# The order of TensorE's steps between two experts' gate and down products: token transposes ahead of and between the halves of down, scatter behind them

## The reference, cut to what matters

```python
def step(acc, xs):
    e, rt, rw = xs
    xb = xf[rt]
    hb = jax.nn.silu(xb @ w_gate[e]) * (xb @ w_up[e])
    yb = (hb @ w_down[e]).astype(F32) * rw[:, None]
    return acc.at[rt].add(yb), None
...
routed = routed_experts(xf, topi, topw, w_gate, w_up, w_down)
shared = (jax.nn.silu(xf @ sh_gate) * (xf @ sh_up)) @ sh_down
return (routed + shared).reshape(B, S, D)
```

## Time and profile before

| | us |
|---|---|
| median of 3 runs | 3258.38 (3256.17 to 3263.91) |
| profiled execution, device time | 3263.08 |
| its span, first to last instruction | 3261.8 |
| TensorE matmuls busy | 2954.0 (91%) |
| VectorE busy | 1182.2 (36%) |
| ScalarE busy | 478.6 (15%) |
| POOL busy | 102.7 (3%) |

### The profile page before, as it was taken

The page is one execution under the profiler, slowest core; times in us unless marked ns, Lnnn a source line. Parts: engine busy times, 40 slices in busy tenths (PEclk is TensorE's granted clock), DMA queues, the critical chain, the costliest instruction groups (busy, mean ns, idle before and its releaser), DMA issues.

```text
span 3261.8 us, 40722 instructions
## 1 busy us (share of the span) xinstructions
PE 2954.0 (91%) x15750; PEld 2104.0 (65%) x15750; DVE 1182.2 (36%) x2590; ACT 478.6 (15%) x1034; POOL 102.7 (3%) x98
## 2 busy tenths in 40 slices
PE   5998899999998899999689999998969689999998
PEld 4766677776666678878475555555858575555554
DVE  1435324433435324441335222224566235222223
ACT  1212210001212301000211111111220111111111
POOL 0000000000000000000001000000000001000000
PEclk9998899999998899999699999999979789999999
DMA  4222135562221146654219999995410119999995
GB/s 153 76 93 76 65 129 207 219 244 101 75 93 71 58 162 225 245 219 154 102 55 376 397 405 405 396 402 230 143 52 1 78 62 411 399 400 392 392 400 233
DMA packets 106612, 684.59 MB, mean 210 GB/s; under 512 B 19777, under 2 KB 21201, under 8 KB 25873
## 3 DMA queue, kind: packets, MB, share of 16 engines
q1 hardware_dynamic: 92384, 661.56, 52.1%
q0 software_dynamic: 11264, 16.54, 1.5%
q10 hardware_dynamic: 2864, 5.09, 0.4%
HBM read 703.57 MB, written 4.19 MB: 217 GB/s over the span
## 4 chain that ended last, share of the span: by engine, by line
PE 76%; DMA 11%; DVE 7%; ACT 3%; issue 1%; ACTq 1%; SPq 0%; DVEq 0%; POOLq 0%
PE PS L440 73%; DMA wmoe<-in_experts 11%; PE PS L445 3%; ACT AR L2013 2%; ACTq L2401 1%; SPq L2529 0%; DVE H L1182 0%; ACT AR L2063 0%; DVE wmoe L1716 0%; DVE H L1716 0%; ACT ST L2013 0%; DVE ST L1235 0%; DMA AR<-tokens,IX 0%; DVE wmoe L1255 0%; ACT wmoe L2013 0%
## 5 line engine op out<-in xcount | busy, mean ns | idle before, releaser
L440 PE MATMUL PS<-wmoe,AR 128*64 128x256 f32 (+1 forms) x5360 | 717.4, 424 | 36.7 <-DMA wmoe<-in_experts 22.6
L440 PE MATMUL PS<-H,wdense 128*128 128x256 f32 (+2 forms) x3056 | 720.5, 397 | 20.8 <-DVE H L1182 9.3
L440 PEld LDWEIGHTS PS<-H,wdense 128*128 128x128 f32 (+1 forms) x3056 | 595.2, 196 | 132.1 <-issue 17.4
L440 PEld LDWEIGHTS PS<-wmoe,AR 128*64 128x64 f32 x5360 | 385.2, 137 | 321.0 <-issue 145.9
L2013 ACT ACTIVATE AR<-PS 128x256 f32<-128x256 f32 (+4 forms) x512 | 231.7, 457 | 1768.4 <-PE PS L440 1159.1
L440 PE MATMUL PS<-AR,wdense 128*128 128x256 f32 (+1 forms) x1920 | 441.0, 391 | 35.7 <-DVE wmoe L1255 10.7
L440 PE MATMUL PS<-AR 128*128 128x512 f32 (+12 forms) x1492 | 413.6, 423 | 57.0 <-DVE AR L1242 13.9
L440 PEld LDWEIGHTS PS<-AR,wdense 128*128 128x128 f32 x1920 | 368.9, 193 | 105.0 <-issue 20.4
L440 PEld LDWEIGHTS PS<-AR 128*128 128x128 f32 (+6 forms) x1492 | 218.0, 200 | 159.5 <-issue 86.6
L445 PEld LDWEIGHTS PS<-CST,AR 128*128 128x128 f32 (+5 forms) x1158 | 132.7, 136 | 178.3 <-issue 137.8
L440 PE MATMUL PS<-wdense,H 128*128 128x256 f32 (+4 forms) x1024 | 219.8, 372 | 0.0
(11 more groups left out here) (286 smaller groups left out, 1580.8 us busy)
## 6 DMA issues: line engine op xcount, KB each, us to landing
wmoe<-in_experts SPq DMA_DIRECT2D x402, 1024.0 KB, 8.7
wdense<-in_dense SPq DMA_DIRECT2D x176, 1024.0 KB, 4.8
wmoe<-in_ada SPq DMA_DIRECT2D x48, 1024.0 KB, 7.0
tokens<-AR POOLq DMA_DIRECT2D x4, 512.0 KB, 3.8
wdense<-in_dense SPq DMA_DIRECT2D x2, 768.0 KB, 11.0
CST<-in_const ACTq DMA_DIRECT2D x1, 1389.0 KB, 20.7
wdense<-in_dense SPq DMA_DIRECT2D x2, 640.0 KB, 6.9
CST<-in_const ACTq DMA_DIRECT2D x1, 1136.0 KB, 15.1
```

Of the source, the lines that this page charges most:

```text
L440: return te.matmul(out, lhsT, rhs, start=start, stop=stop, skip_group_check=True)
```

## The change

The body of a pair is reordered on TensorE. `down` takes one half q at a time. x0 stands between gate_up and the first half of down, x1 between the halves, the first scatter behind the second half, the transposes of the hidden values behind it, then numbers and the second scatter. The event "added before", on which VectorE turns the weights of the last pair, is the second scatter, now the last event of a pair and no longer the one before the last. The other engines' programs are as they were; the counts on which they wait follow the new order.

```diff
-            def down(slots, what):
-                w = [slots(e, 2, D) for e in range(2)]
-                for q in range(2):
-                    for f in range(2):
-                        for e in range(2):
-                            m = mm(PS[e * CAP:(e + 1) * CAP, B_D[q], :], M_HB[:, f, e * CAP:(e + 1) * CAP],
-                                   w[e][:, f, 512 * q:512 * q + 512], start=f == 0, stop=f == 1)
-                    PE.up(m, *what, q)
+            def down(q, w, what):
+                for f in range(2):
+                    for e in range(2):
+                        m = mm(PS[e * CAP:(e + 1) * CAP, B_D[q], :], M_HB[:, f, e * CAP:(e + 1) * CAP],
+                               w[e][:, f, 512 * q:512 * q + 512], start=f == 0, stop=f == 1)
+                PE.up(m, *what, q)
...
-                PE.at[what + ("added before",)] = PE.n - 1
+                PE.at[what + ("added before",)] = PE.n
                 te.wait_ge(AC.sem, at(AC, what + ("x1 read before",)))
                 gate_up(lambda j, k, w: slots(j, k, w), what + ("gu",))
+                te.wait_ge(tokens_landed[L], landings)
+                gather(0, what + ("x0",))
+                w = [slots(4 + e, 2, D) for e in range(2)] if before else None
                 if before:
                     te.wait_ge(AC.sem, at(AC, what + ("turned before",)))
+                    down(0, w, what + ("d",))
+                te.wait_ge(AC.sem, at(AC, what + ("x0",)))
+                gather(1, what + ("x1",))
+                if before:
                     te.wait_ge(VE.sem, at(VE, what + ("numbers before",)))
-                    down(lambda j, k, w: slots(4 + j, k, w), what + ("d",))
-                te.wait_ge(tokens_landed[L], landings)
-                gather(0, what + ("x0",))
-                if before:
+                    down(1, w, what + ("d",))
                     te.wait_ge(VE.sem, at(VE, what + ("ye", 0)))
                     add_up(0, what + ("added",))
-                te.wait_ge(AC.sem, at(AC, what + ("x0",)))
-                gather(1, what + ("x1",))
+                te.wait_ge(VE.sem, at(VE, what + ("hidden",)))
+                turn_hidden(what + ("hb",))
                 te.wait_ge(VE.sem, at(VE, what + ("chosen",)))
                 if before:
                     te.wait_ge(VE.sem, at(VE, what + ("ye", 1)))
                 numbers(p + 2, *what, "numbers")
                 if before:
                     add_up(1, what + ("added",))
-                te.wait_ge(VE.sem, at(VE, what + ("hidden",)))
-                turn_hidden(what + ("hb",))
```

## The result

| | before | after |
|---|---|---|
| median of 9 runs each, us | 3265.98 (3256.17 to 3269.04) | 3277.66 (3272.91 to 3280.78) |
| ratio | | 1.0036, 95% interval 1.0023 to 1.0049 |
| span of the profiled execution, us | 3261.8 | 3276.3 |
| TensorE busy, us | 2954.0 | 2994.3 |

What follows compares the result with a forecast made beforehand. TensorE was busy 91% of the time, the expert layers at DMA share 0.98 and 0.95. Crossings (floor 16.11 us) and token wait (16.5) gave 16.4 us a pair, 65 x 0.2 = +13 us on 3258.4: 3271 us, 3265 to 3287.

Steps and rivals of the forecast that it cites:

- The number: Median of the whole kernel: 3271 us, bounds 3265 to 3287; forecast case given 0.50.
- The unwaited pair: TensorE's expert pair without a wait: two added round trips, 0.48 us, take it from 15.63 to 16.11 us.
- The crossing: Going between 64-column expert products and 128-column work: 0.15 us over, 0.09 back, 0.24 a round trip.
- The new wait: x0 ahead of down waits for gathered tokens: start 7.4 us (7.0 to 7.9) into the pair, against 6.84.
- The path behind the start of down: TensorE's rest of a pair from the start of down products: 8.59 us, against 8.79 before.
- The queues: SP's down refill, issued after d1 about a microsecond later, is covered; ScalarE's and VectorE's copies lie under TensorE's work.
- The sum: Expert loops: mean pair 16.4 us, +0.2 us over 65 pairs, +13 us.
- The signs: Profile after: token waits in over half the pairs, smaller weight wait, unwaited pair 16.1, spacing 16.3 to 16.5, lower DMA share.
- DMA sets the pace: Rival: expert loads set the pair's pace, TensorE's order costs nothing; 3258 us (3252 to 3265), chance 0.22.
- Tokens become the chain: Rival: late x0 delays d1, refill and next gather; +0.5 us a pair, +33 us, 3291; chance 0.10.
- The wait is used: Rival: tokens land in time, x0 lies under the down-weights wait; 13 us faster, 3245; chance 0.18.

Runs made afterwards that it cites:

- x1_behind: Changed kernel with x1 moved from between the down halves to behind both, x0 still ahead of down; ratio 0.9975 to before.
- light_before: Kernel before with expert refills cut from 2048 to 1792 columns a row, stale weights left in the rest; ratio 0.9884 to before.
- rest_between: Changed kernel with all 128-column work between gate/up and down, scatters being those of the pair before; 3267.59 against 3264.48 us, ratio 1.0006 to before.
- light_after: Changed kernel with expert refills cut to 1792 columns a row, stale weights left in the rest; ratio 1.0012 to before.
- light_deferred: x1_behind with the second scatter moved to the next pair ahead of x0, and refills cut to 1792 columns; 3247.2 us, ratio 0.9949 to before.

## Why the prediction was right, point by point

*The number.* 3271 us was forecast, 3277.66 measured, inside 3265 to 3287. Most of the 6.7 us is the kernel before, whose median is 3265.98 over nine runs and was 3258.38 over the three that the forecast stood on; the step is +13 forecast, +11.7 measured.

*The unwaited pair.* The crossing was the right term and too small. I read 0.15 us going over and 0.09 back, 0.24 a round trip, and predicted 16.11; the pair is 16.27, two round trips of 0.32, and the runs with one, two, three and four give 15.63, 15.93, 16.27 and 16.58 (16.68 less 0.10 for the added transpose). The way back was under-read: I had 0.09 from the start of the first expert product alone, and the pieces give more. Down takes 3.58 us in one piece behind one way back (x1_behind) and 2 x 1.87 = 3.74 in two halves with a way back each (1.87 us is the first half in after; the second is the same work): 0.16 us. With the 0.15 of going over that is 0.31, the value that the added transpose gives. The rule of the Trainium skill on changing the tiling mode (TensorEngine Tiling (Array Packing), section Key Properties) agrees with this: each change costs, 0.31 us a round trip by the pair of runs with the added transpose. This trace doesn't show what TensorE does in that time.

*The new wait.* The place was right and the size was not: this is the step of the sum that failed. The working let tokens hold x0 to 7.4 us after the pair's start, 0.56 late, and took half of it, 0.29 a pair above the 16.11. The matmuls lost 0.04 a pair, in 3 of 29 pairs. Two readings did it. The gathers land in 7.1 us, not 7.9: the loads run ahead of TensorE, and theirs too land sooner (median 7.6 us instead of 8.6 in 1722 to 2200). And gate and up take 7.05 us (9.22 less the 2.17 of numbers and second scatter), not 6.84: I had taken the 3.65 of down from a pair in which down waited first, where the stream without a wait has 3.44 (10.49 less 7.05). In the pair behind the one shown the gather, issued at 1956.69, 0.73 us ahead of the first gate product at 1957.42, took 7.7 us, and x0's load started at 1964.47, 0.1 us after it had landed: the tokens come just in time, in most pairs. The other rule, that a semaphore's increment lands after the earlier writes of its DMA engine (DMA: Bandwidth & Descriptors, section Queues, rings and completion order), decided nothing here and is not contradicted: the landing fell together with that of the loads.

*The path behind the start of down.* Predicted 8.59 us; the pieces give 1.87 + 0.59 + 3.78 + 0.22 + 2.17 = 8.63. The gain on the 8.79 of before is 0.16 instead of 0.20. In x1_behind, with no crossing between the halves, it is 3.58 + 0.59 + 1.72 + 0.22 + 2.17 = 8.28, and that kernel is 8 us faster than before.

*The queues.* The later d1 did no harm: the wait for weights went from 11.1 us to none in 1722 to 2200. The trace puts 24 short waits of the weight load at L440 down to ScalarE's copies, 4.3 us in all and 0.4 at most, none of which holds a matmul, and none to VectorE's ye.

*The sum.* Predicted: 16.11 + 0.29 = 16.4 us a pair. Measured: 16.27 + 0.04 = 16.31. The crossings were 0.16 too small and the token wait 0.25 too large, so the near hit of the mean pair is luck, and the step in it, +0.10 (0.12 over the whole loops), is half of the +0.2 forecast. That 11.7 us still stand beside 13 is luck again: about 4 of them are not in the loops. What holds without luck is that the pair grows by its crossings, against a mean that hid 0.58 us of lateness.

*The signs.* Four came: 0.59 at both groups of transposes, a spacing of 16.3, a DMA share a point lower, the wait for weights gone. The pair without a wait read 16.27, not 16.1. Two did not come. Tokens were to be waited for in more than half of the pairs, by about 0.4 us: the PEld line looks like it, with 12 waits of 0.5, but the matmuls waited in 3. And gathers landing by 7.0 us after the pair's start were named as a sign of being wrong: issued 0.73 us ahead of the start, as above, and landing in 7.1 in the median, they land at about 6.4. By that sign the part on the tokens was wrong, and it was.

*The rivals.* "DMA sets the pace" was half right and the more instructive: light_before shows that weights cost the kernel before 38 us, and they hide 31 of the 43 us that the reorder costs TensorE. "Tokens become the chain" did not come. "The wait is used" came too, and was outweighed: take one crossing back, and the same idea is 8 us faster than before; move a scatter there as well, and it is 13.

## What to carry to other kernels

Where two engines' loops are nearly level (here 15.6 us of TensorE beside weights that come every 16.2), a reorder pays by what it lets the other side do earlier, so read both floors: one run with lighter transfers gives TensorE's own. Work moved under a wait must be of the kind that stands there already, or be enough of it to pay for the switch; the same four transposes ahead of down gained 8 us with one added round trip of 0.31 us (x1_behind), and the change, which adds a second one, lost 12; a scatter of 1.72 us moved as well, at no further round trip, brought 13. And a wait that is filled may come back at the next refill, as in rest_between: look at when all slots are released, not only at the one that is waited for. Last, a wait of the weight load is not a wait of the matmuls: count the PE lines.

## What was not expected of the hardware

- A change between 64-column and 128-column products and back costs TensorE 0.31 us at the 2.4 GHz level (granted clock 1.00), for a single transpose as for four: 0.41 us for a transpose placed between expert products, 0.10 for the same one beside others.
- The same gather lands sooner when the loads beside it are lighter: median 7.9 us in before (DMA share 0.99), 7.1 in after (0.98), 6.2 in light_before (0.93), 5.3 in light_after (0.89). The share alone doesn't set it: 7.7 us in rest_between at 0.98, 4.9 in light_deferred at 0.92.
- A DMA share of 0.99 over 475 us still hid 0.58 us a pair of lateness (before, 400 GB/s), and 0.98 stood beside no wait for weights at all (after, 397 GB/s, with a longer pair): the share doesn't tell whether weights come late.
